# Partition sums of the modulation vectors: turned and summed on VectorE before one fp32 product, in place of four fp32 products

## The reference

```
c_act = jax.nn.silu(c)                                  # 1 x 1024
for l in range(2):
    mod = c_act @ ada_w[l] + ada_b[l]                   # 1 x 9216, ada_w[l] is 1024 x 9216
    sh1, sc1, g1, sh2, sc2, g2, sh3, sc3, g3 = jnp.split(mod, 9, axis=-1)
    h = modulate(rms_norm(x, norm_ffn1[l]), sh1, sc1)
    x = x + 0.5 * g1 * swiglu_2(h, ffn1_w_in[l], ffn1_w_out[l])
    ...
```

## Time and profile before

| | |
|---|---|
| median of 3 runs | 3406.98 us (3405.28 to 3407.11) |
| the profiled execution | 3407.11 us, its span 3407.1 us |
| TensorE busy | 3249.5 us, 95% of the span |
| VectorE, ScalarE busy | 1721.4 us (51%), 1250.5 us (37%) |
| mean granted TensorE clock | 0.960 |

### The profile page before, as it was taken

The page is one execution under the profiler, slowest core; times in us unless marked ns, Lnnn a source line. Parts: engine busy times, 40 slices in busy tenths (PEclk is TensorE's granted clock), DMA queues, the critical chain, the costliest instruction groups (busy, mean ns, idle before and its releaser), DMA issues.

```text
span 3407.1 us, 39390 instructions
## 1 busy us (share of the span) xinstructions
PE 3249.5 (95%) x14426; PEld 2633.0 (77%) x14426; DVE 1721.4 (51%) x2652; ACT 1250.5 (37%) x1750; POOL 62.5 (2%) x90
## 2 busy tenths in 40 slices
PE   7899999998999999999988999999999998899998
PEld 5788888766788878888766688887888776678887
DVE  6555426555655256543776465434332568543324
ACT  3343323364434234332323344323442332444421
POOL 0000000000000000000000000000000000000000
PEclk8899999989999999999996899999999999899999
DMA  3365333201455316532321245322333322023321
GB/s 110 93 197 189 94 99 95 92 5 54 144 179 166 97 64 197 184 104 93 90 62 31 68 155 194 122 93 87 97 94 99 91 75 68 7 81 98 98 93 68
DMA packets 262762, 351.61 MB, mean 103 GB/s; under 512 B 16392, under 2 KB 208136, under 8 KB 262664
## 3 DMA queue, kind: packets, MB, share of 16 engines
q1 hardware_dynamic: 240768, 270.57, 25.5%
q0 software_dynamic: 21216, 79.30, 7.1%
q10 hardware_dynamic: 680, 0.43, 0.0%
HBM read 349.87 MB, written 2.10 MB: 103 GB/s over the span
## 4 chain that ended last, share of the span: by engine, by line
PE 84%; DVE 10%; ACT 3%; issue 2%; DMA 0%; SPq 0%; ACTq 0%; DVEq 0%
PE bank L1286 27%; PE bank L1288 26%; PE bank L1287 26%; DVE w_lo L785 2%; PE bank L1545 1%; DVE a_score L1076 1%; DVE a_m L1070 1%; ACT w_hi L518 1%; PE bank L1354 1%; DVE sumsq L794 1%; ACT probs L674 1%; DVE work L823 1%; DVE h_lo L829 1%; PE bank L1328 0%; DVE bank L1107 0%
## 5 line engine op out<-in xcount | busy, mean ns | idle before, releaser
L785 DVE TENSOR_TENSOR w_lo<-raw,w_hi 128x1024 fp32r<-128x1024 f32 x508 | 622.2, 1225 | 1420.8 <-ACT w_hi L518 1420.4
L1286 PE MATMUL bank<-h_hi,w_hi 128*128 128x512 f32 x2928 | 1158.8, 396 | 22.4 <-DVE w_lo L785 15.7
L1287 PE MATMUL bank<-h_lo,w_hi 128*128 128x512 f32 x2928 | 1148.1, 392 | 0.0
L1288 PE MATMUL bank<-h_hi,w_lo 128*128 128x512 f32 x2928 | 1147.6, 392 | 0.0
L518 ACT ACTIVATE w_hi<-raw 128x1024 fp32r<-128x1024 f32 x508 | 537.4, 1060 | 1447.9 <-PE bank L1288 1443.9
L1286 PEld LDWEIGHTS bank<-h_hi,w_hi 128*128 128x128 f32 x2928 | 555.7, 190 | 149.2 <-issue 31.0
L1288 PEld LDWEIGHTS bank<-h_hi,w_lo 128*128 128x128 f32 x2928 | 554.7, 189 | 118.3
L1287 PEld LDWEIGHTS bank<-h_lo,w_hi 128*128 128x128 f32 x2928 | 556.0, 190 | 114.0
L1286 PE MATMUL bank<-act_hi,w_hi 128*128 (+1 forms) x1120 | 440.9, 394 | 0.0
L1288 PE MATMUL bank<-act_hi,w_lo 128*128 (+1 forms) x1120 | 439.2, 392 | 0.0
L1287 PE MATMUL bank<-act_lo,w_hi 128*128 (+1 forms) x1120 | 434.9, 388 | 0.0
(11 more groups left out here) (195 smaller groups left out, 2337.9 us busy)
## 6 DMA issues: line engine op xcount, KB each, us to landing
raw<-in_ffn_w_in_dram SPq DMA_DIRECT2D x176, 512.0 KB, 3.5
ada_w<-in_ada_w_dram POOLq DMA_DIRECT2D x72, 1024.0 KB, 5.6
raw<-in_ffn_w_out_dram SPq DMA_DIRECT2D x88, 512.0 KB, 3.6
raw<-in_ffn_w_gate_dram SPq DMA_DIRECT2D x44, 512.0 KB, 3.9
raw<-in_ffn_w_up_dram SPq DMA_DIRECT2D x44, 512.0 KB, 3.8
raw<-in_ffn_w_down_dram SPq DMA_DIRECT2D x44, 512.0 KB, 3.7
raw<-in_mix_w_in_dram SPq DMA_DIRECT2D x44, 512.0 KB, 3.6
raw<-in_attn_w_qkv_dram SPq DMA_DIRECT2D x24, 512.0 KB, 3.5
```

The lines of the kernel that those rows point to most:

```text
L785: V.tensor_tensor(w_lo[:, nb % SPL, :], raw[:, nb % RAW, :], w_hi[:, nb % SPL, :].bitcast(F32), ALU.subtract).then_inc(s_lo, 1)
L1286: T.matmul(dst, wh, mh, start=first, stop=False)
L1287: T.matmul(dst, wh, ml, start=False, stop=False)
L1288: return T.matmul(dst, wl, mh, start=False, stop=last)
```

## The change

VectorE turns ada_acc in blocks of 32x32 (`V.transpose`), so that in each block of 32 partitions the 32 values which belonged to different partitions of one column lie side by side. It then sums each run of 32 along the free axis: 16 columns (`ada_cols`, 128x16), each with four quarter sums. One fp32 product with a constant 128x128 operand (`quarter_sum`, with a one wherever two partitions have the same place within their block of 32) adds the four quarters and spreads the result. `mod` is then read from it with four additions of 32 partitions each. The constant is built once at the start, in place of a tile of `squares` that has been copied before. TensorE waits for the new semaphore `s_adacols` in place of `s_adastep`. The turn and the sum stand in VectorE's order behind `split_lo(nb + 5, i)`.

```diff
+        quarter_sum = squares[:, 1, :]
+        ada_turned = place("ada_turned", [P, S // 32, 32], at=sq_at)
+        ada_cols = place("ada_cols", [P, S // 32], at=sq_at + S * 4)
...
                     split_lo(nb + 4, i)
                     split_lo(nb + 5, i)
+                    if ada:
+                        dve.wait_ge(s_adastep, 8 * N_MOD * f + 8 + 8 * i)
+                        V.transpose(ada_turned[:].rearrange("p b r -> p (b r)"), ada_acc[:]).then_inc(s_adaturn, 1)
+                        dve.wait_ge(s_adaturn, N_MOD * f + 1 + i)
+                        V.tensor_reduce(ada_cols[:], ada_turned[:], AX_X, ALU.add).then_inc(s_adacols, 1)
                     dve.wait_ge(s_alo, aa + 2 * i)
...
                     if ada:
                         dve.wait_ge(s_adamm, N_MOD * f + 1 + i)
-                        V.tensor_tensor(mod[:, bass.ds(i * 4 + 4 * N_MOD * f, 4)], bank[6][:, 0:4],
-                                        adab[:, bass.ds(i * 4 + 4 * N_MOD * f, 4)], ALU.add).then_inc(s_mod, 1)
+                        for r in range(4):
+                            rows = slice(32 * r, 32 * r + 32)
+                            ins = V.tensor_tensor(mod[rows, bass.ds(i * 4 + 4 * N_MOD * f, 4)],
+                                                  bank[6][rows, 0:S // 32].rearrange("p (j r) -> p r j", r=4)[:, r, :],
+                                                  adab[rows, bass.ds(i * 4 + 4 * N_MOD * f, 4)], ALU.add)
+                        ins.then_inc(s_mod, 1)
...
             V.tensor_copy(turn_hi[:], squares[:, 1:3, :]).then_inc(s_ones, 1)
+            dve.wait_ge(s_ones, 3)
+            link(V.tensor_reduce(quarter_sum[:, 0:32], ident.rearrange("p (g c) -> p c g", c=32), AX_X, ALU.add))
+            link(V.tensor_copy(quarter_sum[:, 32:P].rearrange("p (n c) -> p n c", c=32),
+                               quarter_sum[:, 0:32].unsqueeze(1).to_broadcast([P, 3, 32])))
             split_lo(0)
             split_lo(1)
...
                     if ada:
-                        pe.wait_ge(s_adastep, 8 * N_MOD * f + 8 + 8 * i)
+                        pe.wait_ge(s_adacols, N_MOD * f + 1 + i)
                         if not (f == 0 and first):
                             pe.wait_ge(s_mod, N_MOD * f + i)
-                        for j in range(4):
-                            ins = T.matmul(bank[6][:, j:j + 1], ada_acc[:, j * P:(j + 1) * P], small[:, 66:67],
-                                           start=True, stop=True)
-                        ins.then_inc(s_adamm, 1)
+                        T.matmul(bank[6][:, 0:S // 32], quarter_sum[:], ada_cols[:], start=True, stop=True).then_inc(s_adamm, 1)
```

More of the change, by code:

```diff
@@ L261, in program @@
         s_adastep = sem("ada_partial_sum")
+        s_adaturn = sem("ada_sum_turned")
+        s_adacols = sem("ada_sum_by_quarters")
         s_adamm = sem("ada_reduced")
```

## The result

The changed kernel took 3604.4 us (median of 4 runs, 3601.4 to 3610.8) against 3407.1 us: the ratio is 1.0578 (95% interval 1.0565 to 1.0592), slower by 5.8% or 197 us. The prediction was 3605 us. The profiled execution took 3610.8 us with a span of 3609.1 us.

The account below looks back on a forecast made before the run. The prediction took TensorE's own work, 84% of the chain, to bound the kernel. 3407.1 + 122 (stall) + 76 (clock) + 0.2 (start) = 3605 us, 5.8% slower; 8 in 10 range 3525 to 3670.

Parts of the forecast that it names:

- The stall: TensorE waits at each modulation iteration's fourth slab end for VectorE's reduction: 3.39 us net, times 36 is 122 us.
- the forecast chain: At each modulation iteration's slab end, one after the other: ScalarE's w_hi, VectorE's w_lo, transpose, reduction, product, next slab at 252.57.
- The dear pair: Rival: VectorE's transpose and reduction both at their upper bounds, 2.31 us together, giving 3638 us; chance 9%.
- The estimate of 0.57 us: Alternative price for VectorE's transpose and reduction each: a quarter of 2293 ns for 2048 fp32 elements, making 122 us 114.
- The clock: After each stall TensorE drops to 1.2 GHz: 2.1 us lost per iteration, 76 us over 36; bounds 1.6 and 3.2.
- one long stretch in three: Slow clock after a stall lasts 3.4 us in two iterations of three, otherwise 6.9 us, costing 1.6 or 3.2 us.
- the one counter-example at 2799.3: Earlier trace's 2.6 us TensorE idle without a clock fall; backed the rival that the clock holds, 3529 us, chance 13%.
- The saving: Three of the four small TensorE products removed per modulation iteration: 36 x 0.61 = 22 us saved if run back to back.
- The start: Two small VectorE instructions between turn_hi and the first two w_lo, mostly hidden: 0.2 us, bounds 0 and 1.

Follow-up runs that it names:

- the runs with 1.2 and 2.4 us: The kernel before with one TensorE wait added ahead of its four products: for ScalarE's w_hi of slab nb+5, 3473.3 us; for VectorE's w_lo of it, 3551.2 us.

## Why the prediction was right

**The wait, not the work.** The step that decided was to ask what stands ahead of the turn in VectorE's queue. It held: moving the pair ahead of one w_lo turns +197 us into -28 us, and the wait alone, with no pair, costs 144 us.

**The stall, 3.39 us forecast, 3.65 in the iteration shown, 3.70 on average.** The turn took 0.70 us and the sum 0.69, each forecast at 0.69; from ScalarE's w_hi to the product every start agrees with the forecast chain to 0.02 us. The forecast idle time was 3.74 us, the measured one 3.75 here and 3.80 on average (136.7 / 36). The term that was mis-sized is the last: 0.30 us from the product to the next slab, where it is 0.56. That is 36 x 0.26 = 9 us. It had been worked out as 0.91 less three products of 0.20, from four products outside a loop. Inside the loop four products after a wait take 0.91 too (210.13 to 211.04, in the run with the wait alone), so the subtraction was at fault: four products cover the loop's end, one leaves it bare. The dear pair is out: an upper bound of 2.31 us for the two stood against 1.39 measured. The reductions' slope in the earlier trace rows was one of their strides or shapes, not of the reduction as such; the strided one of 128 elements at the start (0.37 us, below) still lies on it. The estimate of 0.57 us from the tier table of the Trainium skill ("VectorE: DVE Perf Modes", "The perf-mode tier table") was 0.12 us short, since a quarter of the elements takes more than a quarter of the time: a subtraction takes 1.22 us for 1024 elements and 0.69 for 512 (L871 in the kernel before), so an estimated 0.16 us stay whatever the length. The copy's 0.69 was the better price. The advice in the "Rules for kernel authors" of that page of the Trainium skill against tensor_reduce on a hot path did not decide anything, since the same reduction is free one line earlier.

**The clock, 2.1 us forecast, 1.9 measured** (68 us over 36 iterations, from the run with TensorE kept busy). The guess of one long stretch in three gave 4.6 us at 1.2 GHz in each iteration; it was 4.5, with 11 long ones of 36. That idle times shorter than this one had brought the clock down in the earlier trace rows was the right evidence; the one counter-example at 2799.3 fits the runs with 1.2 and 2.4 us, in which the clock falls after some stalls and not after others. What the forecast left out is that some of the low clock costs nothing: 13 of the 160 us pass before the next slab's first product, while TensorE waits for the sum or stands at its loop's end. The other 147 cost 36 x 1.93 = 69 us, 0.47 each, as forecast from the pace. The Trainium skill ("TensorE: Matmul & The Clock Gate", "HAM oscillation — how this bites in real kernels") charges half of all throttled time; by that the 4.5 us would cost an estimated 2.2 in each iteration, 0.3 more than was measured.

**The saving.** 22 us forecast for three products of four, 25 to 28 measured with the pair out of the way, since the remaining product takes 0.14 us and not 0.20.

**The start.** Two small instructions of 0.37 and 0.25 us were forecast to cost 0.2 us. VectorE's timeline of the changed kernel has the first reciprocal 3.29 us after the start of turn_hi, 22.44 to 25.73:

```profile
22.44 0.29 DVE L1211 CAST turn_hi<-squares 128x256 fp32r<-128x256 f32 x1
22.76 0.37 DVE L1213 TENSOR_REDUCE squares<-squares 128x32 f32<-128x128 f32 x1
23.16 0.25 DVE L1214 COPY squares<-squares 128x96 f32<-128x96 f32 x1
...
25.73 0.17 DVE L808 RECIPROCAL sd<-sd 128x4 f32<-128x4 f32 x1
```

In the trace of before the first of the two is

```profile
22.63 0.29 DVE L1196 CAST turn_hi<-squares 128x256 fp32r<-128x256 f32 x1
```

and the second starts at 25.74, 3.11 us later, so the cost is 0.18 us.

**The sum.** 36 x (3.70 + 1.93) + 0.2 = 203 us. The two profiled executions differ by just that (3610.8 less 3407.1 is 203.7), the medians by 197. An iteration was forecast at 28.2 us and takes 28.34 on average. The forecast's 198 rests on two errors of opposite sign, 11 us too little for the stall and 6 too much for the clock, and on a median that lies 6 us below the profiled execution. Within 1 us of the median is luck, the two terms being right to 10% is not.

What stays open: what decides, at a given idle time, after which stalls the clock falls, and for which of the two lengths.

## What to carry to other kernels

Before moving work to an idle engine, read what the engine waits for in that idle time. VectorE was idle half of the span here, but the instruction in front of the new ones was waiting for the very engine that would wait for them, and so 1.4 us of work cost 5.5. The cure is the order within the queue: put work whose inputs are ready ahead of the look-ahead instruction that waits for the bottleneck. And price an idle time of the matrix engine as its length plus the slow pace behind it, here half as much again.

## What the runs showed of the hardware

- A turn in 32x32 blocks of 128x512 fp32 takes 0.70 us and a free-axis sum of 128x512 fp32 0.69 us, both the time of a plain copy out of PSUM (0.69).
- One fp32 product with a 128x128 stationary operand and 16 moving columns takes 0.14 us when TensorE's queue is full. When it starts after a wait it is 0.24 us to the next matmul at the full clock, and 0.56 with the loop's end between the two. With four products of one column in front of it the same loop's end doesn't show (0.91 us inside the loop and outside).
- Idle times of 1.2, 2.4, 3.75 and 5.2 us between full slabs left the granted clock over one block at 0.99, 0.95, 0.92 and 0.89. It fell behind 7, 29, 36 and 36 of the 36 stalls, with 0, 1, 11 and 35 of these falls lasting 6.8 us and the others 3.4. Filling the 3.75 us with useless matmuls left it at 1.00 and gave 68 us back.
